# Feature blocks modulated straight from PSUM, and another order at the start of the output projection

## The reference

```python
mod_x = (silu_c @ w_ada[l] + b_ada[l])[:, None, :]      # six parts: shift, scale, gate, twice
mod_c = silu_cc @ w_ada[l] + b_ada[l]
hx = rmsnorm(x, norm1_g[l]) * (1.0 + sc1x) + sh1x       # latent tokens
hc = rmsnorm(xc, norm1_g[l]) * (1.0 + sc1c) + sh1c      # context tokens
p_c, p_x = prepare_mixers(hc, ...), prepare_mixers(hx, ...)
oc_gla, oc_gdn, ctx_states = run_mixers(p_c, None)      # both directions, from zero state
ox_gla, ox_gdn, _ = run_mixers(p_x, ctx_states)         # each from the context's final state
x = x + gt1x * merge_heads(ox_gla, ox_gdn, p_x, gla_norm_g[l], gdn_norm_g[l], w_out[l], x.dtype)
```

## Time and profile before

| | us |
|---|---|
| median of 3 runs | 1767.58 (1764.86 to 1772.41) |
| the profiled execution | 1768.08 |
| its span in the trace | 1766.3 |
| mean granted clock of TensorE | 0.959 |
| busy: PE, DVE, ACT, POOL | 1582.8, 1011.2, 653.3, 403.3 |

### The profile page before, as it was taken

How to read it: one execution, slowest core, us unless ns; L and a number is a source line. 1 busy time by engine, 2 the same in 40 slices (tenths; PEclk the granted TensorE clock), 3 DMA queues, 4 the chain that set the end, 5 groups by cost and what they waited for, 6 DMA issues and landing times. The chain is left out here.

```text
span 1766.3 us, 35611 instructions
## 1 busy us (share of the span) xinstructions
PE 1582.8 (90%) x15222; PEld 1345.5 (76%) x15222; DVE 1011.2 (57%) x1553; ACT 653.3 (37%) x991; POOL 403.3 (23%) x353
## 2 busy tenths in 40 slices
PE   7799999999978888888875898699999989899997
PEld 6567887999978777777775787578888867787886
DVE  4344542111116777777776656745455588887975
ACT  6476345221112222222223224545455553233333
POOL 0002110111104545554545111322232200000000
PEclk9799999999989989998998999899999999999999
DMA  9213333526545333333322322044444587163522
GB/s 315 74 54 114 114 98 99 152 84 193 175 136 141 94 110 110 110 109 110 110 62 90 114 90 96 28 131 163 161 132 149 173 303 262 59 227 119 167 84 96
DMA packets 179518, 229.95 MB, mean 130 GB/s; under 512 B 34237, under 2 KB 112321, under 8 KB 179362
## 3 DMA queue, kind: packets, MB, share of 16 engines
q1 hardware_dynamic: 172850, 206.85, 36.4%
q0 software_dynamic: 6512, 20.84, 3.8%
HBM read 165.91 MB, written 61.73 MB: 129 GB/s over the span
## 5 line engine op out<-in xcount | busy, mean ns | idle before, releaser
L87 PE MATMUL fps<-xh_m,w1r_hi 128*128 128x512 f32 x448 | 178.5, 398 | 18.7 <-DVE w1r_lo L2679 5.8
L87 PE MATMUL fps<-bh,ah 128*128 128x512 f32 x448 | 176.6, 394 | 13.9 <-DVE acc L2832 9.4
L88 PE MATMUL fps<-xl_m,w1r_hi 128*128 128x512 f32 x448 | 176.7, 394 | 0.0
L89 PE MATMUL fps<-xh_m,w1r_lo 128*128 128x512 f32 x448 | 176.4, 394 | 0.0
L88 PE MATMUL fps<-bl,ah 128*128 128x512 f32 x448 | 176.1, 393 | 0.0
L89 PE MATMUL fps<-bh,al 128*128 128x512 f32 x448 | 176.0, 393 | 0.0
L80 PE MATMUL ps_main<-hhi,whi 128*128 128x512 f32 (+1 forms) x336 | 128.1, 381 | 3.9 <-ACT lr_x L773 3.9
L82 PE MATMUL ps_main<-hhi,wlo 128*128 128x512 f32 (+1 forms) x336 | 124.5, 371 | 0.0
L81 PE MATMUL ps_main<-hlo,whi 128*128 128x512 f32 (+1 forms) x336 | 124.3, 370 | 0.0
L2479 ACT ACTIVATE ah<-araw 128x2048 fp32r<-128x2048 f32 x28 | 53.7, 1917 | 185.4 <-PE fps L89 121.0
L80 PE MATMUL ps_main<-whi,hhi 128*128 128x256 f32 x416 | 120.4, 289 | 0.0
(11 more groups left out here) (319 smaller groups left out, 3615.3 us busy)
## 6 DMA issues: line engine op xcount, KB each, us to landing
s_hid<-hb SPq DMA_DIRECT2D x112, 256.0 KB, 2.3
araw<-s_hid SPq DMA_DIRECT2D x28, 1024.0 KB, 6.7
w1raw<-in_w_ff SPq DMA_DIRECT2D x16, 1024.0 KB, 6.4
w2b<-in_w_ff SPq DMA_DIRECT2D x16, 1024.0 KB, 6.6
raw<-in_w_in SPq DMA_DIRECT2D x14, 1024.0 KB, 5.4
z_sb<-in_w_ada SPq DMA_DIRECT2D x16, 512.0 KB, 4.4
n_sb<-in_w_ada SPq DMA_DIRECT2D x16, 512.0 KB, 4.3
kc<-s_k SPq DMA_DIRECT2D x20, 256.0 KB, 3.3
```

The costliest lines, as they stand in the source:

```text
L87: pe.matmul(out, lhi, rhi, start=start, stop=False, skip_group_check=True)
L88: pe.matmul(out, lhi, rlo, start=False, stop=False, skip_group_check=True)
L89: return pe.matmul(out, llo, rhi, start=False, stop=stop, skip_group_check=True)
```

## The change

In modulation, all ten diagonals are kept (`diag` has ten places), and `turn` goes by feature blocks: ten products of block k for ten tiles into three PSUM banks, two blocks at a time. `full` reads PSUM and writes one of three buffers `hf`: VectorE 1024 tokens of an even block and 512 of an odd one, ScalarE the rest. The copies to `xt` are gone. The turn of blocks 2 and 3 stands behind `select(1)` on TensorE, and so on. W_ada has three slots; its groups 3 and 4 wait for `columns` to have used slots 0 and 1. The tiles of x are loaded in another order beside them. In mixing, VectorE's steps 2 to 4 get one backward context scan each and step 5 the copy. In merging these scans are gone, the variance operation is gone (the logarithm takes scale and bias instead), all remainders but two are VectorE's, the preparation of tiles 0 and 1 is interleaved with the weights' remainders in another order, and tile 0's product goes in two halves over the feature blocks, with tile 1's turn between them.

The diff, cut to its core (of modulation's and of the last product's orders only the new lines stand, the old ones are in the listing above):

```diff
-        TOGETHER = ((0, 1), (1, 1), (2, 2), (4, 2), (6, 2), (8, 2))
+        TOGETHER = ((0, 2), (2, 2), (4, 2), (6, 2), (8, 2))
-        xt = m.sb("xturn", [P, KT, NTOK])
+        hf = m.sb("hf", [P, NB, NTOK])
+        wa = m.sb("wa", [P, 3, 4 * D])
+        wslot = [x.rearrange("p (z k n) -> p z k n", z=2, k=KT) for x in
+                 (wa[:, 0], wa[:, 1], wa[:, 2], wa[:, 0, :2 * D], wa[:, 1, :2 * D])]
-        wa = m.sb("wa", [P, 2, 4 * D])
-        wslot = [x.rearrange("p (z k n) -> p z k n", z=2, k=KT) for x in
-                 (wa[:, 0], wa[:, 1], *(xs[:, a:b].rearrange("p t d -> p (t d)") for a, b in ((0, 4), (4, 6), (6, 8))))]
-        diag = K.gt2[:, 512:1024].rearrange("p (x n) -> p x n", n=P)
+        diag = m.sb("diag", [P, NT, P])
...
-        ps_cols = m.ps("ps_cols", [P, 512])
-        ps_t = m.ps("ps_t", [P, 4, 512])
+        ps_t = m.ps("ps_t", [P, 2, 3, 512])
...
-        PIECES = [(0, 0, HALF), (1, 0, HALF), (0, HALF, NTOK), (1, HALF, NTOK), (2, 0, NTOK), (3, 0, NTOK), (4, 0, NTOK),
-                  (5, 0, NTOK), (6, 0, NTOK), (7, 0, HALF), (7, HALF, NTOK)]
-        BY_ACT = (1, 3, 5, 6)
...
-            sp.dma_start(xs[:, 0], xr[0]).then_inc(ld_x[0], 16)
+            for t in range(3):
+                sp.dma_start(xs[:, t], xr[t]).then_inc(ld_x[t], 16)
             sp.dma_start(K.ident[:], A["k_ident"]).then_inc(ld_const, 16)
-            for t in range(1, 4):
-                sp.dma_start(xs[:, t], xr[t]).then_inc(ld_x[t], 16)
+            sp.dma_start(xs[:, 3], xr[3]).then_inc(ld_x[3], 16)
...
-            for t in range(4, 6):
+            for t in range(4, 8):
                 sp.dma_start(xs[:, t], xr[t]).then_inc(ld_x[t], 16)
             load_w(0)
-            for t in range(6, NT):
+            for t in range(8, NT):
                 sp.dma_start(xs[:, t], xr[t]).then_inc(ld_x[t], 16)
             load_w(1)
-            for g, last in ((2, 3), (3, 5), (4, 7)):
-                sp.wait_ge(t_ready, 2 * last + 2)
-                load_w(g)
+            load_w(2)
+            sp.wait_ge(w_used, 1)
+            load_w(3)
+            sp.wait_ge(w_used, 2)
+            load_w(4)
...
+            def full(k):
+                act.wait_ge(t_ready, k + 1)
+                act.wait_ge(sc1_done, group_of(k) + 1)
+                if k >= NB:
+                    act.wait_ge(lo_done, k - NB + 1)
+                if k % 2:
+                    act.activation(hf[:, k % NB, HALF:NLAT], ps_t[:, k % 2, 1], ACT.Identity, scale=sc1[:, k, 0:1],
+                                   bias=K.mod[:, k, 0:1]).then_inc(hf_act, 1)
+                act.activation(hf[:, k % NB, NLAT:], ps_t[:, k % 2, 2, :NCTX], ACT.Identity, scale=sc1[:, k, 1:2],
+                               bias=K.mod[:, k, 1:2]).then_inc(hf_act, 1)
+
+            def high(k, lo, hi):
+                act.wait_ge(hf_dve, k + 1)
                 roots(r)
+                act.activation(K.hhi[:, k, lo:hi], hf[:, k % NB, lo:hi], ACT.Copy).then_inc(hi_done, 1)
+
+            for r in range(4):
                 roots(r)
             row(0)
+            roots(4)
+            act.wait_ge(ss_done, NT)
+            full(0)
             full(1)
+            high(0, 0, NTOK)
+            high(1, 0, NTOK)
+            row(1)
+            full(2)
             full(3)
+            high(2, 0, NTOK)
+            high(3, 0, NTOK)
+            row(2)
+            full(4)
             full(5)
+            high(4, 0, NTOK)
+            row(3)
+            high(5, 0, NTOK)
+            full(6)
+            row(4)
+            high(6, 0, NTOK)
             full(7)
+            high(7, 0, HALF)
+            high(7, HALF, NTOK)
...
             def diagonal(r):
                 t0, n = TOGETHER[r]
+                q = slice(t0, t0 + n)
+                dve.wait_ge(ss_done, t0 + n)
+                dve.tensor_scalar(var[:, q], ss[:, q], 1.0 / D, EPS, ALU.mult, ALU.add).then_inc(var_done, 1)
                 dve.wait_ge(rstd_done, r + 1)
                 if r == 0:
                     dve.wait_ge(ld_const, 16)
                 for t in range(t0, t0 + n):
-                    if t >= 4:
-                        dve.wait_ge(t_ready, 2 * (t - 3))
-                    dve.tensor_scalar(diag[:, t % 4], K.ident[:], rstd[:, t:t + 1], None, ALU.mult).then_inc(diag_done, 1)
...
+            def full(k):
+                dve.wait_ge(t_ready, k + 1)
+                n = 1 if k % 2 else 2
+                dve.tensor_scalar(hf[:, k % NB, :n * HALF], ps_t[:, k % 2, 0:n].rearrange("p b n -> p (b n)"), sc1[:, k, 0:1],
+                                  K.mod[:, k, 0:1], ALU.mult, ALU.add).then_inc(hf_dve, 1)
+
+            def low(k, lo, hi):
+                dve.wait_ge(hi_done, k + 1 + (lo > 0))
+                dve.tensor_tensor(K.hlo[:, k, lo:hi], hf[:, k % NB, lo:hi], K.hhi[:, k, lo:hi].bitcast(F32),
                                   ALU.subtract).then_inc(lo_done, 1)

...
+            for r in range(4):
+                diagonal(r)
             dve.wait_ge(ld_sel, 16)
             dve.tensor_reduce(sel2[:], K.sel[:, 0:8].rearrange("p (n v) -> p v n", v=2), AX.X, ALU.add).then_inc(sel_done, 1)
+            dve.wait_ge(cols_ready, 1)
+            dve.tensor_copy(K.cols[:], ps_mod[:, COLS]).then_inc(cols_done, 1)
+            scales(0)
             diagonal(4)
             full(0)
+            full(1)
+            low(0, 0, NTOK)
+            low(1, 0, NTOK)
+            scales(1)
             full(2)
+            full(3)
+            low(2, 0, NTOK)
+            low(3, 0, NTOK)
+            scales(2)
             full(4)
+            full(5)
+            low(4, 0, NTOK)
+            scales(3)
             full(6)
+            low(5, 0, NTOK)
+            low(6, 0, NTOK)
             scales(4)
+            full(7)
+            low(7, 0, HALF)
+            low(7, HALF, NTOK)
...
+            def turn(k):
+                if k >= 2:
+                    pe.wait_ge(hf_dve, k - 1)
+                    pe.wait_ge(hf_act, k - 1 + (k - 1) // 2)
+                for t in range(NT):
+                    if k == 0:
+                        pe.wait_ge(diag_done, t + 1)
+                    last = pe.matmul(ps_t[:, k % 2, t // 4, (t % 4) * P:(t % 4 + 1) * P], xs[:, t, k * P:(k + 1) * P], diag[:, t],
+                                     start=True, stop=True)
+                last.then_inc(t_ready, 1)
...
+            pe.transpose(ps_mod[:, COLS], rows[:100, :], K.ident[:100, :100]).then_inc(cols_ready, 1)
             pe.wait_ge(pad_done, 1)
             pe.wait_ge(c_silu, 1)
             columns(0)
             select(0)
+            turn(0)
+            turn(1)
+            columns(1)
+            select(1)
+            turn(2)
+            turn(3)
+            columns(2)
+            select(2)
+            turn(4)
+            turn(5)
+            columns(3)
+            select(3)
             turn(6)
+            columns(4)
+            select(4)
             turn(7)
...
+            def context_back(i):
+                to = 2 * TC - 2 - i
+                if i:
+                    dve.wait_ge(scan_back, 2 * i)
+                for a in R2:
+                    dve.scalar_tensor_tensor(K.ga_st[:, to, 1, a], K.ga_st[:, to + 1, 1, a], K.ga_a[:, to, 1, a:a + 1],
+                                             K.ga_st[:, to, 1, a], ALU.mult, ALU.add).then_inc(scan_back, 1)
+
+            def context_end():
+                dve.wait_ge(scan_back, 2 * (2 * TC - 1))
+                dve.tensor_copy(K.ga_st[:, 2 * NT, 1], K.ga_st[:, 0, 1])

...
                     advance(p)
+                    if TC <= p < 3 * TC - 1:
+                        context_back(p - TC)
+                    if p == 3 * TC - 1:
+                        context_end()
...
+            pool.memset(eps[:], EPS).then_inc(eps_done, 1)
+            gate(0)
             low_w(1)
-            gate(0)
+            gate(1)
             low_w(3)
-            low_w(5)
-            gate(1)
...
-                act.wait_ge(var_done, t + 1)
-                act.activation(lnv[:], var[:], ACT.Ln).then_inc(ln_done, 1)
+                act.wait_ge(ss_done, t + 1)
+                if t == 0:
+                    act.wait_ge(eps_done, 1)
+                act.activation(lnv[:], ss[:], ACT.Ln, scale=1.0 / P, bias=eps[:]).then_inc(ln_done, 1)
                 act.wait_ge(ln_done, t + 1)
...
             for k in range(3):
                 high_w(k)
+            square(0)
             for x in range(2):
                 act.wait_ge(rows_done, x + 1)
                 act.activation(K.gt2[:, x * 512:(x + 1) * 512], ps_p[:, x], ACT.Copy).then_inc(row_out, 1)
-            square(0)
+            rsqrt(0)
+            square(1)
             high_w(3)
-            rsqrt(0)
             high_w(4)
+            high(0)
+            rsqrt(1)
             high_w(5)
-            square(1)
             high_w(6)
             high_w(7)
-            rsqrt(1)
-            high(0)
             for t in range(TL):
                 if t + 2 < TL:
...
```

(86 more changed lines are left out.)

177 lines of the change are left out of this document (26 added, 151 removed).

## The result

The changed kernel takes 1771.82 us (median of 17 runs, 1763.7 to 1776.2), the kernel before in the same comparison 1765.40 (17 runs, 1760.5 to 1773.8). The ratio is 1.0029, with an interval of 1.0017 to 1.0041: about 5 us slower. That is inside the range of 1756 to 1774 and within the half per cent that had most of the chance, but the forecast of 1765.0 has the wrong sign. The profiled execution took 1773.69 us.

A forecast was written before the change was run, and what follows sets the result against it. Modulation was taken as bound by a chain handed between engines, merging's steady part by TensorE alone. Modulation +4.2, ramp -7.2 and mixing 0 gave -3.0 us: 1765.1 by the profiled execution, forecast 1765 us, range 1756 to 1774.

The forecast's parts named there:

- First block ready at 29.8, the second 2.2 later, select(1) at 36.4: Modulation's start: first block waits for the last diagonals at 29.0 and two products; second at 32.0, then ScalarE's 4.4 us.
- A product of a turn is 0.123 (16 in 1.97) at the full one and 0.224 at the low one: Modulation's turns: us per product at full and low clock, giving rounds of 8.1 or 10.9 us, stage end 62.0 or 70.4.
- The chain of ScalarE of 4.4: Modulation, second block's arrival to the next select: scaling 1.31, two roundings 2.41, row 0.57, handover 0.1 us.
- The clock, "up within bursts and down in waits", the middle taken: TensorE's clock in modulation's rounds: stage end taken at 66.1 us, a loss of 4.2.
- my own two ends: Modulation's predicted end: 62.0 us at the full clock, 70.4 at the low one, against 61.89 before.
- Loads don't decide; PSUM reads hidden: Modulation: group 2 lands near 37, before its use at 41; VectorE's pair costs 5.3 us in rounds of at least 8.1.
- Mixing costs nothing: VectorE's steps 2 to 5 in mixing: added scans and copy hide in waits for TensorE, cost 0; unhidden 2.4 us.
- The ramp, 7.9 worked out, 7.2 taken: Merging's start: the new order brings the first output product at 971.4 instead of 979.34 us; low end 5.3.
- The moved queries: Merging's ramp: states_query(2), behind the load of x issued at 964.2, lands near 968; inter(2) ends by 971.1 us.
- The steady part, "nothing is gained": Merging from 992 to 1072 us: TensorE busy 80 of 80 us, so removing the variance operation gains nothing there.
- The sum: Whole kernel: modulation +4.2, ramp -7.2, mixing 0, together -3.0 us, forecast 1765 us.
- Rival (b): Modulation's turns: TensorE stays at 1.2 GHz, 8.5 us lost; slower if select(1) to stage end exceeds 33 us; chance 0.14.

The follow-up runs named there:

- filler: The changed kernel with seven dummy products, results unused, in each of TensorE's waits ahead of selections 1 to 3: ratio 1.0003 to the kernel before, modulation ends at 67.35 us.

## Why the prediction was wrong in its sign, step by step

- **First block ready at 29.8, the second 2.2 later, select(1) at 36.4**: 30.52, 33.31 and 37.40. The numbers are right within 1.3 us, but by luck. I had the first block wait for the last diagonal, at 29.0, and two products. The last diagonal ended at 27.66 (27.18 + 0.48), and what the block waited for was TensorE's own ten products, from 25.86 on at 0.45 each. The second block came 2.8 behind the first, another trace of the error below.
- **"A product of a turn is 0.123 (16 in 1.97) at the full one and 0.224 at the low one" is the step that failed.** It is 0.246 and 0.447 by the same rows, 0.236 in a run of twenty (filler). I read the row's count as products. The turns of the code (ten tiles, one product each), set against the x16 of a turn of one tile's eight blocks, would have shown two records for each. In the filler, at the full clock, the part from select(2) to the scaling of block 5 (47.45 to 53.11) is 5.66, not 3.7, and the round 9.76, not 8.1; the stage ends at 67.35, where 62.0 stood. The price alone is worth 5.75 here, 2.25 for each of two pairs of turns (4.71 against 2.46) and 1.25 for turn(6), against the 5.35 by which the stage's end is late; the other steps were off both ways and nearly cancel.
- **The chain of ScalarE of 4.4**: 4.1 from the second block's arrival to the next selection (44.70 to 48.78). Right.
- **The clock, "up within bursts and down in waits", the middle taken**: the mechanism is right, the size is luck. My 4.2 was the clock's share alone, and by the filler the share behind the waits is 4.0. But with the right price my own two ends would have been about 67.8 and 83.8 (62.0 + 5.75; 70.4 + 13.4, for 60 products at 0.447 instead of 0.224; estimates), and their middle 75.8. The measured 71.84 is nearer to the full clock: the price was half of the true one and the share of the low clock was taken too large.
The Trainium skill (TensorE: Matmul & The Clock Gate, section HAM oscillation) describes a kernel with bursts shorter than the waits between them, whose every burst starts throttled. Here, with bursts longer than the waits, it is so in part: the turns at 38.32 and 50.52 were slowed (6.34 and 7.05 instead of 4.71), that at 60.79 was not (2.48 for ten).
- **Loads don't decide; PSUM reads hidden**: right. The 20 copies taken out bought nothing, as the time between selections is the chain's.
- **Mixing costs nothing**: right, the wait for TensorE shrank from 0.94 to 0.42. Ten profiles with the scans in mixing average 435.5 us for it, four without them 436.1.
- **The ramp, 7.9 worked out, 7.2 taken**: 8.35 in the pair of profiles, in which the first products ran at 1.2 GHz before (3.58) and at the full clock after (2.02). The moved queries behaved as argued: states_query(2) issues 11.5 us after the stage's start (before: 6.6), and inter(2) is the last to end before the output. VectorE's scaling did run into GpSimd's remainder (3.36 instead of 1.22).
- **The steady part, "nothing is gained", was costed at nothing and lost 2.0**: the step missing is the placing of the new tile, which the diff shows and the prediction doesn't mention, so that it stood at nothing without a reason. No row of before could give its price.
- **The sum** was +4.2 - 7.2 = -3.0. With the measured terms it is +10.5 - 8.4 + 2.0 = +4.1, against 5.1 measured. Rival (b), slower through TensorE's turns, had the right place and the right deciding point: select(1) to the stage's end took 34.4 us against its 33. Its mechanism, 1.2 GHz from the first turn on, was there only in part: in the changed kernel's profile pairs of turns took 7.41, 6.34 and 7.05, where 4.71 is the price at the full clock, and the single turns 2.48, which is that price. What it lacked is that a product costs twice as much at either clock.

## What to carry to other kernels

Before a row's count is used as a divisor, set it against the number of instructions that the code issues in that stretch: a price that is wrong by two turned the sign of this forecast. When copies are taken off a chain, ask what work of TensorE now stands between two waits, and whether that work needs the wait at all: giving it the idle time ahead of the selection, by reordering alone, was worth 11 us, more than the ramp's whole gain. When a new small tile is put ahead of tiles that TensorE reads, look up where these then start: here 32 bytes cost 2 us. Whether other tiles mind it is not shown.

## What the runs showed of the hardware

- The place in SBUF of the 128x128 operand tiles sets the pace of these fp32r products of 512 columns: 0.2275 us with `yhi` at byte 212928 of a partition, 0.233 with it at 212960, 32 bytes further (2.5%; nine profiles against five). The weight loads' own records don't change (188 ns in both).
- With TensorE's waits of 2.3 us filled by dummy products the granted clock was 1.00 in every 5 us from 35 to 65, where it had been 0.50 to 0.86 from 35 to 55; the 21 dummies, 5.5 us of TensorE's time, took 4.0 us off the stage (one profile against the mean of seven).
- The granted clock can read 1.00 where products run at the price of 1.2 GHz: 0.45 us each from 25.86 to 30.4, as from 50.52 to 55.1 under a clock of 0.50, against 0.236 in the filler.
- An operation of VectorE on 8 values takes 1.07 to 1.25 us in the ramp, where it waits for the sum of squares ahead of it and GpSimd has a remainder under way (the like of it on 2 values took 0.17 in modulation); on the path it cost only 0.2 to 0.8 us.
